# Softmax attentions with row sums from the value matmul and operand copies by DMA, in a two-block transformer step

## Chip, core and metric

The kernel runs on one core of a Trainium2 chip. The metric is the device time of one execution in microseconds (us).

## What is computed

Sequence 512, width 1024, batch 1, all in float32. The first block is one layer with two attention branches, a stick-breaking attention ("sb", 8 heads) and a latent attention ("mla", 8 heads of width 96, softmax over chunks of 64); the second has a softmax attention with forget-gate decay ("fox", 16 heads of 64), a short convolution, and two wide MLPs. The change touches the two softmax attentions. Cut to these:

```python
# mla: chunk-causal softmax, then the gate
z = einsum("bhqd,bshd->bhqs", q_blk, k) * scale
p = softmax(where(allowed, z, -inf), axis=-1)
o = einsum("bhqs,bshd->bhqd", p, v)
y_mla = (o * silu(gate_mla)) @ w_o_mla

# fox: causal softmax with cumulative log decay c
s = einsum("bhqd,bhkd->bhqk", q * HEAD_DIM ** -0.5, k)
s = s + c[..., :, None] - c[..., None, :]
s = where(k_pos <= q_pos, s, NEG_INF)
o = einsum("bhqk,bhkd->bhqd", softmax(s, axis=-1), v)
m = o @ w_out
```

## The kernel before, in words

Every product is made of split operands: a number is a high part (ScalarE's rounded copy) plus a low part (VectorE's difference), and `three` (L702 to L704) issues three matmuls for one product. Weights come in units of 1 MB: SP loads a unit into one of two raw slots (`load`, L490 and L491; it waits until the unit two places earlier has been split, `w_split`), ScalarE writes the high part (`w_hi`), VectorE the low part (`w_split`). Each engine runs its own stream in order, and semaphores alone tie the streams together.

The two softmax attentions run over pairs of heads: MLA 4 pairs, fox 8. What an engine does in a pair is written out by hand as an order of steps, one string for each engine (`PE_MLA`, `ACT_FOX` and so on; the last two pairs have strings of their own, `..._LAST`). A step is a letter and a number; for heads 0 and 1 of the pair the numbers 0 to 3 and 4 to 7 are query blocks of 128 rows, which see 128, 256, 384 and 512 keys:

- z: PE, scores of a block and the mask into one of three banks (L960, L964). For block 0 or 4 it waits until the head is staged.
- m: VectorE, negated row maximum (L1983). e: ScalarE, exponential with the row sum in an accumulator (L1412).
- n: VectorE, reciprocal of the sum (L1988) and P times it (L1991).
- t: PE, transposes of the block of P (L972). For s of 2 and more it waits for p of s - 2, since two banks take turns.
- p: high part of the turned P on ScalarE (L1421), low part on VectorE (L1694).
- v: PE, value product of a head, 12 matmuls, after p of its fourth block.
- g on PE: a share (6 matmuls of 512 columns) of a projection that runs beside, `beside`; its result is taken by x on VectorE (L1848) after the eighth share. u: the same for a second unit in the last pair.
- g on VectorE: `gather`, the head's output out of bank 5, in MLA times the gate (L1857, L1859).
- w on ScalarE, c on VectorE: the split of the unit beside which comes next, in two halves (L1190) and four quarters (L1658). c0 waits for `w_hi` of the whole unit, which w1 gives; `w_split` comes with c3.
- s on both: `stage` of the coming head, s1 of the pair's second head, s2 of the next pair's first. ScalarE writes high parts (L1288 to L1302), VectorE low parts. In fox ScalarE also writes second copies of q and k into the other half of the operand, and the decay rows picked out of `ssum` (L1293, L1294, L1298).
- o: split of a finished output tile for the output projection.

A fox pair p (0 to 7) has the unit `fox_qk_next` number p beside it in pairs 0 to 5 and splits number p + 1; pairs 6 and 7 have the output projection beside them. SP loads these units in a loop that holds nothing else. Behind the attention PE does the shares left of the output projection.

Of the kernel before, what the change touches and what calls it, by code (L numbers as in the profile page):

```python
# [208 lines left out]
def hybrid_block_kernel(nc, ins, out):  # L209
# [4 lines left out]
    with ctx:  # L214
        def sb(name, shape, dt=F32):
            return ctx.enter_context(nc.sbuf_tensor(name, shape, dt))
# [2149 lines left out]
```

## Time and profile before

| | us |
|---|---|
| median of 3 runs | 1865.53 (1863.59 to 1865.70) |
| profiled execution, time | 1864.47 |
| its span, first to last instruction | 1862.7 |
| PE busy | 1764.2 (95%) |
| VectorE busy | 1110.9 (60%) |
| ScalarE busy | 750.5 (40%) |
| GpSimd busy | 179.4 (10%) |
| granted clock of TensorE, mean | 0.986 |

The profile is one execution. Its times run from the span's start; the MLA attention lies at 324 to 415 us, the fox attention at 567 to 770. A matmul's row has its start and a modelled end, and a busy PE counts overlapping matmuls once. A window's row gives the stretch, its length, each engine's busy time with its number of instructions, the granted TensorE clock (1.00 is full speed), the mean busy share of the DMA engines and GB/s. "Idle before" is the idle time of an engine ahead of an instruction, with what ended it.

### The profile page before, as it was taken

The numbers are of one execution on the slowest core, as the hardware profiler recorded it, in microseconds if no ns is written. First come the engines' busy times: TensorE is split into PE (matmuls) and PEld (weight loads), VectorE is DVE, ScalarE is ACT, GpSimd is POOL, SyncE is SP. The second block draws the span as 40 slices with busy tenths as digits, with TensorE's granted clock in tenths as the row PEclk, the third lists the DMA queues.
The fourth block names the chain that finished last, engine by engine and source line by source line (L and its number), as shares of the span: only waits on it lengthen the run. The fifth ranks groups of instructions, "written<-read, shape, count | busy, mean of one in ns | idle before, by whom it ended". The sixth has DMA issues, their size and how long they took to land.

```text
span 1862.7 us, 22288 instructions
## 1 busy us (share of the span) xinstructions
PE 1764.2 (95%) x8332; PEld 1439.5 (77%) x8332; DVE 1110.9 (60%) x1580; ACT 750.5 (40%) x1169; POOL 179.4 (10%) x144
## 2 busy tenths in 40 slices
PE   8999999999898887989999999889999999999987
PEld 6988876888697675768888888667887788888866
DVE  6467767886556777675444453776556635354465
ACT  4266673554425667352222222642224322122245
POOL 2001110000300000140000001430003100000041
PEclk9999999999999998999999999989999999999999
DMA  7312133114231110223223222213222322322221
GB/s 248 95 48 68 48 70 102 46 46 137 67 91 46 46 45 1 91 68 113 90 97 106 90 91 95 86 45 113 94 99 68 114 90 96 106 91 90 86 68 62
DMA packets 162477, 156.23 MB, mean 84 GB/s; under 512 B 13602, under 2 KB 157247, under 8 KB 162143
## 3 DMA queue, kind: packets, MB, share of 16 engines
q1 hardware_dynamic: 162398, 155.16, 26.4%
q8 instruction: 52, 0.85, 0.2%
q14 instruction: 27, 0.21, 0.0%
HBM read 150.36 MB, written 4.19 MB: 83 GB/s over the span
## 4 chain that ended last, share of the span: by engine, by line
PE 65%; issue 13%; DVE 10%; ACT 5%; POOL 4%; DMA 1%; POOLq 0%; SPq 0%; DVEq 0%; ACTq 0%
PE bank L702 20%; PE bank L704 20%; PE bank L703 20%; POOL ssum L2296 3%; PE bank L972 1%; DVE act_b L1694 1%; PE bank L960 1%; DVE split_weights L1650 1%; DVE work L1709 1%; DVE negmax L1983 1%; POOL tmp L2329 1%; DVE act_a L1696 1%; DVE tmp L1991 1%; ACT split_weights L1181 1%; DMA raw_weights<-in_w_ple_gate 1%
## 5 line engine op out<-in xcount | busy, mean ns | idle before, releaser
L702 PE MATMUL bank<-act_a,split_weights 128*128 128x512 f32 x1392 | 557.5, 400 | 29.3 <-DVE act_a L1696 28.9
L704 PE MATMUL bank<-act_a,split_weights 128*128 128x512 f32 x1392 | 546.6, 393 | 0.0
L703 PE MATMUL bank<-act_a,split_weights 128*128 128x512 f32 x1392 | 546.0, 392 | 0.0
L1181 ACT ACTIVATE split_weights<-raw_weights 128x2048 fp32r<-128x2048 f32 (+1 forms) x119 | 223.7, 1880 | 343.7 <-PE bank L704 343.7
L1650 DVE TENSOR_TENSOR split_weights<-raw_weights,split_weights 128x2048 fp32r<-128x2048 f32 (+1 forms) x119 | 275.7, 2317 | 124.0 <-ACT split_weights L1181 120.6
L702 PEld LDWEIGHTS bank<-act_a,split_weights 128*128 128x128 f32 x1392 | 263.3, 189 | 94.0 <-issue 23.8
L704 PEld LDWEIGHTS bank<-act_a,split_weights 128*128 128x128 f32 x1392 | 262.7, 189 | 57.5
L703 PEld LDWEIGHTS bank<-act_a,split_weights 128*128 128x128 f32 x1392 | 263.3, 189 | 53.6 <-issue 2.2
L702 PE MATMUL bank<-act_b,split_weights 128*128 128x512 f32 x664 | 260.4, 392 | 0.0
L703 PE MATMUL bank<-act_b,split_weights 128*128 128x512 f32 x664 | 258.4, 389 | 0.0
L704 PE MATMUL bank<-act_b,split_weights 128*128 128x512 f32 x664 | 258.4, 389 | 0.0
L2300 POOL TENSOR_TENSOR ssum<-sq 128x512 f32<-128x512 f32 x16 | 28.0, 1750 | 1256.0 <-ACT sq L1211 1252.7
L702 PEld LDWEIGHTS bank<-act_b,split_weights 128*128 128x128 f32 x664 | 124.7, 188 | 26.8 <-issue 1.2
L703 PEld LDWEIGHTS bank<-act_b,split_weights 128*128 128x128 f32 x664 | 124.7, 188 | 26.8 <-issue 1.2
L704 PEld LDWEIGHTS bank<-act_b,split_weights 128*128 128x128 f32 x664 | 124.7, 188 | 26.0
L1518 ACT ACTIVATE act_b<-tmp 128x512 fp32r<-128x512 f32 x64 | 40.3, 632 | 229.3 <-DVE tmp L2157 227.9
L1211 ACT ACTIVATE sq<-work 128x512 f32<-128x512 f32 x117 | 71.0, 625 | 147.6 <-DVE work L2176 58.1
L2157 DVE SCALAR_TENSOR_TENSOR tmp<-bank,rstd 128x512 f32<-128x512 f32 x64 | 43.6, 691 | 137.2 <-PE bank L704 136.3
L2296 POOL TENSOR_TENSOR ssum<-ssum,sq 128x512 f32<-128x512 f32 x77 | 109.1, 1417 | 156.9 <-ACT sq L1211 148.5
L2176 DVE TENSOR_TENSOR work<-bank,work 128x512 f32<-128x512 f32 x48 | 32.9, 692 | 120.0 <-PE bank L704 120.0
L1694 DVE TENSOR_TENSOR act_b<-tmp,act_b 128x512 fp32r<-128x512 f32 (+3 forms) x136 | 77.4, 605 | 10.7 <-ACT act_b L480 9.3
L1412 ACT ACTIVATE tmp<-bank,negmax 128x128 f32<-128x128 f32 (+1 forms) x96 | 50.4, 526 | 56.3 <-DVE negmax L1983 56.3
(193 smaller groups left out, 2126.0 us busy)
## 6 DMA issues: line engine op xcount, KB each, us to landing
raw_weights<-in_w_mlp_up SPq DMA_DIRECT2D x32, 1024.0 KB, 5.4
raw_weights<-in_w_mlp_down SPq DMA_DIRECT2D x32, 1024.0 KB, 5.1
raw_weights<-in_w_in SPq DMA_DIRECT2D x20, 1024.0 KB, 5.3
raw_weights<-in_w_conv_in SPq DMA_DIRECT2D x12, 1024.0 KB, 5.1
raw_weights<-in_w_attn_in SPq DMA_DIRECT2D x16, 512.0 KB, 4.5
raw_weights<-in_w_ple_gate SPq DMA_DIRECT2D x8, 1024.0 KB, 5.2
raw_weights<-in_w_out SPq DMA_DIRECT2D x4, 1024.0 KB, 5.1
raw_weights<-in_w_attn_in SPq DMA_DIRECT2D x4, 1024.0 KB, 5.2
```

Source lines behind the costliest of these rows:

```text
L702: nc.tensor.matmul(dst, w[0], a[0], start=first, stop=False)
L703: nc.tensor.matmul(dst, w[0], a[1], start=False, stop=False)
L704: mm = nc.tensor.matmul(dst, w[1], a[0], start=False, stop=last)
L1181: nc.scalar.activation(wsp[:, pl.slot, 0, pl.split_cols], raw[:, pl.slot, pl.raw_cols], ACT.Copy)\
L1211: nc.scalar.activation(sq[:, parity, :], src, ACT.Square).then_inc(sq_done, 1)
L1412: nc.scalar.activation(tmp[:, s % 4, 0:(j + 1) * P], score_bank(s, last)[:, 0:(j + 1) * P], ACT.Exp, bias=negmax[:, s:s + 1], accum_out=ro ...
L1518: nc.scalar.activation(act_b[:, 0, 2 * j + m, :], tmp[:, m, :], ACT.Square)\
L1650: V.tensor_tensor(wsp[:, pl.slot, 1, cols], raw[:, pl.slot, pl.raw_cols], wsp[:, pl.slot, 0, cols].bitcast(F32), ALU.subtract).then_inc(w_ ...
L1694: V.tensor_tensor(dst, src, hi.bitcast(F32), ALU.subtract).then_inc(sem_, 1)
L2157: V.scalar_tensor_tensor(out=tmp[:, m, :], in0=done(pl, m)[:, :], scalar=0.0, in1=rstd[:, :], op0=ALU.max, op1=ALU.mult).then_inc(tile_rea ...
L2176: V.tensor_tensor(t, done(pl, m)[:, :], t, ALU.add).then_inc(tile_read, 1)
L2296: nc.gpsimd.tensor_tensor(ssum[:, :], ssum[:, :], sq[:, parity, :], ALU.add).then_inc(sq_added, 1)
```

## The change

Row sums and normalisation. `head_v` becomes twice as wide, V's 64 columns and 64 more that hold 1.0 in the high part and 0.0 in the low part, set once. The value product then has 128 output rows: rows 64 to 127 of bank 5 are the row sums, 64 times. P is turned as the exponential gives it. A new step r on ScalarE (`invert_sums`) takes Ln and Exp with scale -1 of the sums into a half of `sq`, and `gather` multiplies by that; in MLA the gate is a multiplication of its own for both heads.

Staging in fox. ScalarE makes three copies a head instead of six (`HI_STEPS` 3). SP makes the second copies of q and k and the two decay rows with four DMAs a head (`copy_halves`), and PE waits for them (`halves_copied`) at the head's first scores.

The orders of all engines in MLA and fox are written anew (the PE orders of the last two fox pairs stay).

```diff
-        head_v = sb("head_v", [P, 2, 2, TT, HD], F32R)
+        head_v = sb("head_v", [P, 2, 2, TT, 2 * HD], F32R)
-        HI_STEPS = {"sb": 4, "mla": 3, "fox": 6}
+        HI_STEPS = {"sb": 4, "mla": 3, "fox": 3}
-        PE_MLA = "z0 z1 g0 z2 t0 g1 z3 t1 g2 z4 t2 z5 g3 t3 z6 t4 z7 v0 t5 g4 g5 t6 t7 g6 g7 v1"
-        PE_FOX = "z0  z1 g0 z2 t0 g1 z3 t1 g2 z4 t2 z5 g3 t3 z6 t4 z7 v0 t5 g4 g5 t6 t7 g6 g7 v1"
-        ACT_MLA = "s1 e0 e1 e2 p0 e3 p1 w0 e4 p2 e5 p3 w1 e6 s2 p4 p5 e7 p6 p7"
-        ACT_FOX = "s1  e0 e1 e2 p0 e3 p1 w0 e4 p2 e5 p3 w1 e6 s2 p4 p5 e7 p6 p7"
-        DVE_MLA = "m0 m1 n0 s1 m2 n1 m3 n2 p0 p1 n3 m4 m5 p2 n4 p3 n5 m6 c0 n6 m7 c1 p4 c2 g0 n7 p5 c3 s2 p6 p7 x0 x1 g1"
-        DVE_FOX = "m0  m1 n0 s1 m2 n1 m3 n2 p0 p1 n3 m4 m5 p2 n4 p3 n5 m6 c0 n6 m7 c1 p4 c2 g0 n7 p5 c3 s2 p6 p7 x0 x1 g1"
+        PE_MLA = "z0 z1 z2 g0 g1 t0 z3 g2 t1 z4 t2 z5 g3 t3 z6 g4 v0 t4 z7 t5 g5 t6 t7 g6 g7 v1"
+        ACT_MLA = "s1 e0 e1 p0 e2 w0 w1 p1 p2 e3 e4 p3 e5 e6 s2 r0 p4 p5 e7 p6 p7 r1"
+        DVE_MLA = "m0 m1 m2 s1 p0 m3 c0 m4 p1 m5 c1 p2 c2 p3 m6 m7 p4 p5 p6 g0 p7 s2 x0 x1 c3 g1"
+        PE_FOX = "z0 z1 z2 g0 g1 t0 z3 t1 g2 z4 t2 t3 z5 g3 t4 v0 z6 t5 z7 g4 g5 t6 t7 g6 g7 v1"
+        ACT_FOX = "s1 e0 e1 p0 e2 p1 e3 p2 p3 e4 e5 s2 p4 p5 w0 e6 e7 r0 p6 p7 w1 r1"
+        DVE_FOX = "m0 m1 m2 s1 m3 p0 p1 m4 p2 p3 m5 s2 m6 p4 m7 p5 c0 c1 g0 p6 p7 x0 c2 x1 c3 g1"
-        ACT_LAST = ("s1 e0 e1 e2 o0 p0 w0 e3 o1 p1 p2 o2 w1 e4 e5 p3 s2 e6 p4 e7 p5 p6 p7 o3",
-                    "s1 e0 e1 e2 o4 p0 p1 e3 o5 e4 p2 p3 e5 e6 p4 p5 o6 e7 p6 p7")
-        DVE_LAST = ("m0 n0 m1 m2 n1 s1 n2 m3 p0 o0 m4 p1 n3 m5 o1 p2 p3 n4 c0 m6 n5 o2 g0 n6 c1 p4 m7 c2 n7 p5 s2 c3 p6 p7 o3 g1",
-                    "m0 m1 n0 m2 s1 n1 n2 o4 p0 p1 m3 m4 n3 m5 o5 n4 p2 p3 n5 m6 n6 m7 g0 p4 n7 o6 p5 p6 p7 g1")
-        ACT_MLA_LAST = "e0 s1 e1 e2 p0 e3 p1 w0 e4 p2 e5 p3 w1 e6 p4 e7 p5 o0 o1 p6 p7 o2"
-        DVE_MLA_LAST = "m0 m1 n0 s1 m2 n1 m3 p0 n2 p1 m4 n3 m5 p2 n4 p3 n5 m6 c0 n6 m7 c1 p4 c2 g0 n7 p5 c3 o0 p6 o1 p7 x0 x1 o2 g1"
+        ACT_LAST = ("s1 e0 e1 e2 o0 p0 w0 e3 o1 p1 p2 o2 w1 e4 e5 p3 s2 e6 p4 r0 e7 p5 p6 p7 o3 r1",
+                    "s1 e0 e1 e2 o4 p0 p1 e3 o5 e4 p2 p3 e5 e6 p4 p5 r0 o6 e7 p6 p7 r1")
+        DVE_LAST = ("m0 m1 m2 s1 m3 p0 o0 m4 p1 m5 o1 p2 p3 c0 m6 o2 c1 p4 m7 g0 c2 p5 s2 c3 p6 p7 o3 g1",
+                    "m0 m1 m2 s1 o4 p0 p1 m3 m4 m5 o5 p2 p3 m6 m7 p4 p5 g0 o6 p6 p7 g1")
+        ACT_MLA_LAST = "s1 e0 e1 p0 e2 w0 w1 p1 p2 e3 e4 p3 e5 e6 r0 p4 o0 p5 e7 o1 p6 p7 o2 r1"
+        DVE_MLA_LAST = "m0 m1 m2 s1 p0 m3 c0 m4 p1 m5 c1 p2 c2 p3 m6 m7 p4 o0 p5 g0 o1 p6 c3 p7 x0 x1 o2 g1"
             loop("fox_v", 2, 2, lambda i, j: attn_in[:, :, bass.ds(2 * D + 512 * i + 256 * j, 256)])
-            with sp.Fori(0, 3) as i:
-                for j in range(2):
-                    load_qk(Place(tab, "fox_qk_next", j, i, 2, 3), 2 + 2 * i + j)
+            def copy_halves(h):
+                hh = h % 2
+                qk, (own, other) = qk_parts("fox", hh), halves(hh)
+                sp.wait_ge(ATT["fox"]["stage_hi"], HI_STEPS["fox"] * h + 2)
+                for dst, src in ((qk(0)[other, :], qk(0)[own, :]), (qk(3)[own, :], qk(2)[own, :])):
+                    sp.dma_start(dst.bitcast(F32), src.bitcast(F32)).then_inc(halves_copied[hh], 16)
+                for part in range(2):
+                    row, to = 32 * part + h, other.start + part
+                    sp.dma_start(qk(3)[to:to + 1, :].bitcast(F32), ssum[row:row + 1, :]).then_inc(halves_copied[hh], 16)
             for j in range(2):
-                pl = Place(tab, "fox_out", j)
-                load_out(pl, j)
+                load_qk(Place(tab, "fox_qk_next", j), 2 + j)
+            sp.wait_ge(forget_log, 4)
+            sp.wait_ge(pad_zero, 3)
+            copy_halves(0)
+            load_qk(Place(tab, "fox_qk_next", 2), 4)
+            for pair in range(FOX_HEADS // 2):
+                copy_halves(2 * pair + 1)
+                if pair < 3:
+                    load_qk(Place(tab, "fox_qk_next", 3 + pair), 5 + pair)
+                elif pair < 5:
+                    load_out(Place(tab, "fox_out", pair - 3), pair - 3)
+                if pair < FOX_HEADS // 2 - 1:
+                    copy_halves(2 * pair + 2)
...
                     if j == 0:
                         pe.wait_ge(A["staged"], 3 * (2 * i + hh) + 3)
+                        if kind == "fox":
+                            pe.wait_ge(halves_copied[hh], 64 * i + 64)
...
                 def turn(i, s):
-                    pe.wait_ge(A["normed"], 8 * i + s + 1)
+                    pe.wait_ge(A["exp"], 8 * i + s + 1)
...
-                        three(banks[5][0:HD, c:S], [head_v[:, hh, hl, kt, :] for hl in (0, 1)],
+                        three(banks[5][:, c:S], [head_v[:, hh, hl, kt, :] for hl in (0, 1)],
...
-                if kind == "fox":
-                    nc.scalar.activation(qk(0)[other, :], q, ACT.Copy, scale=scale).then_inc(A["stage_hi"], 1)
-                    nc.scalar.activation(qk(3)[own, :], k, ACT.Copy).then_inc(A["stage_hi"], 1)
-                    if first:
-                        act.wait_ge(pad_zero, 3)
-                    pick = consts[0:48, bass.ds(ccols["sel"].start + 2 * i + hh, 1)]
-                    nc.scalar.activation(qk(3)[other.start:other.start + 48, :], decay_parts, ACT.Copy, scale=pick)\
-                        .then_inc(A["stage_hi"], 1)
...
-                                         bias=negmax[:, s:s + 1], accum_out=rowsum[:, s:s + 1]).then_inc(A["exp"], 1)
+                                         bias=negmax[:, s:s + 1]).then_inc(A["exp"], 1)
+
+                def invert_sums(i, hh):
+
+                    h = 2 * i + hh
+                    act.wait_ge(A["out"], FREE + h + 1)
+                    nc.scalar.activation(sum_inverse(hh), banks[5][HD:2 * HD, :], ACT.Ln).then_inc(A["sum_log"], 1)
+                    act.wait_ge(A["sum_log"], h + 1)
+                    nc.scalar.activation(sum_inverse(hh), sum_inverse(hh), ACT.Exp, scale=-1.0).then_inc(A["sum_inverse"], 1)
...
-                if kind == "fox":
-                    V.tensor_scalar(dst, src, 1.0, None, ALU.mult).then_inc(A["gathered"], 1)
+                if kind != "sb":
+                    dve.wait_ge(A["sum_inverse"], 2 * i + hh + 1)
+                    V.tensor_tensor(dst, src, sum_inverse(hh), ALU.mult).then_inc(A["gathered"], 1)
+                    if kind == "mla" and hh == 1:
+                        dve.wait_ge(A["gathered"], FREE + 2 * i + 2)
+                        V.tensor_tensor(output_tile(kind, i), output_tile(kind, i), wt(TILES[kind]["gate"] + i), ALU.mult)\
+                            .then_inc(A["gated"], 1)
...
-                def normalize(i, s):
-                    dve.wait_ge(A["exp"], 8 * i + s + 1)
-                    V.reciprocal(rinv[:, s:s + 1], rowsum[:, s:s + 1]).then_inc(A["step"], 1)
-                    dve.wait_ge(A["step"], 8 * i + s + 1)
-                    t = tmp[:, s % 4, 0:(s % TT + 1) * P]
-                    V.tensor_scalar(t, t, rinv[:, s:s + 1], None, ALU.mult).then_inc(A["normed"], 1)
```

## Rows read from the trace of the kernel before

**Rows 1.** The page's busy time of each engine, its share of the span, instructions
```profile
PE 1764.2 (95%) x8332; PEld 1439.5 (77%) x8332; DVE 1110.9 (60%) x1580; ACT 750.5 (40%) x1169; POOL 179.4 (10%) x144
```

**Rows 2.** Table of windows, one MLA pair, then fox pairs 0, 1, 2, 6, 7
```profile
core 0: us, PE busy (x) PEld busy (x) DVE busy (x) ACT busy (x) POOL busy (x), PEclk, DMA share, GB/s
324.00:346.60 22.60, 22.11 (x124) 18.52 (x125) 18.04 (x45) 13.11 (x34) 0.00 (x0) 1.00 0.19 58
...
567.30:595.00 27.70, 22.92 (x115) 18.24 (x116) 18.74 (x45) 19.35 (x43) 0.00 (x0) 0.94 0.15 39
595.00:619.40 24.40, 21.56 (x118) 17.11 (x117) 19.16 (x46) 16.45 (x38) 0.00 (x0) 1.00 0.15 40
619.40:645.20 25.80, 22.99 (x118) 18.36 (x117) 19.35 (x46) 16.43 (x38) 0.00 (x0) 0.93 0.17 45
...
718.50:745.80 27.30, 18.57 (x89) 13.95 (x88) 20.37 (x48) 18.39 (x42) 0.00 (x0) 0.81 0.00 1
745.80:770.00 24.20, 21.12 (x110) 16.59 (x107) 15.93 (x41) 9.65 (x28) 0.00 (x0) 0.93 0.34 109
```

**Rows 3.** Waits of PE, 595 to 717: waiter, releaser, us in total, times, longest
```profile
PE bank L972 <- DVE act_b L1694: 11.3, 10, 1.6
```

**Rows 4.** Lines by form, VectorE, one fox pair: count, busy us, mean ns, idle before
```profile
L1988 DVE RECIPROCAL rinv<-rowsum 128x1 f32<-128x1 f32 x8 | 1.2, 155 | 0.3 <-ACT tmp L1412 0.2
...
L1991 DVE TENSOR_SCALAR tmp<-tmp,rinv 128x512 f32<-128x512 f32 x2 | 1.0, 488 | 0.1
...
L1991 DVE TENSOR_SCALAR tmp<-tmp,rinv 128x128 f32<-128x128 f32 x2 | 0.6, 286 | 0.1
```

**Rows 5.** Lines by form, ScalarE, the same fox pair
```profile
L1190 ACT ACTIVATE split_weights<-raw_weights 128x1024 fp32r<-128x1024 f32 x2 | 2.1, 1054 | 0.0
L1412 ACT ACTIVATION_READ_ACCUMULATOR tmp<-bank,negmax 128x1 f32 x8 | 1.6, 197 | 0.0
...
L1421 ACT ACTIVATE act_b<-bank 128x512 fp32r<-128x512 f32 x2 | 1.2, 598 | 2.3 <-PE bank L972 2.3
...
L1298 ACT ACTIVATE act_b<-ssum,consts 48x512 fp32r<-48x512 f32 x1 | 0.7, 723 | 0.0
...
L1293 ACT ACTIVATE head_qk<-work 64x512 fp32r x1 | 0.6, 632 | 0.0
```

**Rows 6.** Timeline of SP, 589.0 to 590.5: start, us, DMAs issued
```profile
589.32 1.00 SPq L491 DMA_DIRECT2D raw_weights<-in_w_attn_in  x2
```

**Rows 7.** Timeline of SP, 286 to 292: start, us, DMAs issued
```profile
286.64 4.95 SPq L569 DMA_DIRECT2D work<-tmp  x8
```

**Rows 8.** The page's DMA issues: count, KB each, median us from issue to landing
```profile
work<-tmp SPq DMA_DIRECT2D x8, 64.0 KB, 2.0
```

**Rows 9.** DMA view, 589.0 to 595.0: busy tenths in 40 slices
```profile
DMA  0000000002664779999999999999999999610200
```

**Rows 10.** Timeline of VectorE, 658 to 670: start, us, operation
```profile
662.04 0.68 DVE L1658 TENSOR_TENSOR split_weights<-raw_weights,split_weights 128x512 fp32r<-128x512 f32 x1
662.64 0.68 DVE L1857 TENSOR_SCALAR work<-bank 64x512 f32 x1
...
666.53 1.15 DVE L1694 TENSOR_TENSOR act_b<-bank,act_b 128x384 fp32r<-128x384 f32 x2
```

**Rows 11.** Timeline of PE, 1230 to 1244: start, us, [idle before <-releaser]
```profile
1238.24 0.76 PE L702 MATMUL bank<-act_a,split_weights 128*128 128x512 f32 x1 [6.04 <-DVE act_a L1696]
1238.80 0.63 PE L703 MATMUL bank<-act_a,split_weights 128*128 128x512 f32 x1
1239.22 0.63 PE L704 MATMUL bank<-act_a,split_weights 128*128 128x512 f32 x1
...
1243.76 0.39 PE L703 MATMUL bank<-act_a,split_weights 128*128 128x512 f32 x1
1243.98 0.40 PE L704 MATMUL bank<-act_a,split_weights 128*128 128x512 f32 x1
```

**Rows 12.** Table of windows, columns as in rows 2
```profile
1238.20:1243.50 5.30, 5.26 (x13) 4.13 (x14) 5.30 (x6) 2.67 (x6) 2.73 (x2) 0.50 0.00 0
```

More of the change, by code:

```diff
@@ L246, in hybrid_block_kernel @@
         negmax = sb("negmax", [P, 8])
-        rowsum = sb("rowsum", [P, 8])
-        rinv = sb("rinv", [P, 8])
         banks = [ctx.enter_context(nc.psum_tensor(f"bank{i}", [P, S], F32)) for i in range(8)]
@@ L337, in hybrid_block_kernel @@
                 "part_ready", "summed", "w_exp", "negmax", "exp", "normed", "pt_hi", "pt_ready",
-                "out", "gathered", "o_hi", "o_ready", "step")}
+                "out", "sum_log", "sum_inverse", "gathered", "gated", "o_hi", "o_ready")}
+        halves_copied = [sem("halves_copied0"), sem("halves_copied1")]
         block = ctx.enter_context(nc.Block())
@@ L427, in halves, with sum_inverse @@
             return slice(hh * HD, (hh + 1) * HD), slice((1 - hh) * HD, (2 - hh) * HD)
+        def sum_inverse(hh):
+            return sq[hh * HD:(hh + 1) * HD, 0, :]
         def head_values(kind, i, hh):
@@ L908, in _ @@
                         c = min(kt * P, S - 2 * P)
-                        three(banks[4 + hh][0:HD, c:S], [head_v[:, hh, hl, kt, :] for hl in (0, 1)],
+                        three(banks[4 + hh][0:HD, c:S], [head_v[:, hh, hl, kt, 0:HD] for hl in (0, 1)],
                               [act_b[:, hl, kt, c:S] for hl in (0, 1)], kt == 0, kt == TT - 1,
@@ L1291, in stage @@
                     nc.scalar.activation(qk(2)[other, :], k, ACT.Copy).then_inc(A["stage_hi"], 1)
-                if kind == "fox":
-                    nc.scalar.activation(qk(0)[other, :], q, ACT.Copy, scale=scale).then_inc(A["stage_hi"], 1)
-                    nc.scalar.activation(qk(3)[own, :], k, ACT.Copy).then_inc(A["stage_hi"], 1)
-                    if first:
-                        act.wait_ge(pad_zero, 3)
-                    pick = consts[0:48, bass.ds(ccols["sel"].start + 2 * i + hh, 1)]
-                    nc.scalar.activation(qk(3)[other.start:other.start + 48, :], decay_parts, ACT.Copy, scale=pick)\
-                        .then_inc(A["stage_hi"], 1)
                 if not first:
                     act.wait_ge(A["out"], FREE + 2 * i + hh - 1)
-                nc.scalar.activation(head_v[:, hh, 0, :, :], head_values(kind, i, hh), ACT.Copy).then_inc(A["stage_hi"], 1)
+                nc.scalar.activation(head_v[:, hh, 0, :, 0:HD], head_values(kind, i, hh), ACT.Copy).then_inc(A["stage_hi"], 1)
             table("sigmoid_and_others")
@@ L1349, in output_hi @@
             def output_hi(kind, k):
-                act.wait_ge(ATT[kind]["gathered"], FREE + 2 * k + 2)
+                if kind == "mla":
+                    act.wait_ge(ATT[kind]["gated"], k + 1)
+                else:
+                    act.wait_ge(ATT[kind]["gathered"], FREE + 2 * k + 2)
                 nc.scalar.activation(out_parts(kind, 0, k), output_tile(kind, k), ACT.Copy).then_inc(ATT[kind]["o_hi"], 1)
@@ L1435, in two_pairs @@
                                 output_hi(kind, s)
+                            elif what == "r":
+                                invert_sums(pair, s)
                             elif what == "e":
@@ L1820, in stage @@
                 dve.wait_ge(A["stage_hi"], before + HI_STEPS[kind])
-                low(head_v[:, hh, 1, :, :], head_values(kind, i, hh), head_v[:, hh, 0, :, :], A["staged"])
+                low(head_v[:, hh, 1, :, 0:HD], head_values(kind, i, hh), head_v[:, hh, 0, :, 0:HD], A["staged"])
             def rest_halves(part, value):
@@ L1836, in _ @@
                     rest_halves(3, 0.0)
+                    for hl, value in ((0, 1.0), (1, 0.0)):
+                        V.memset(head_v[:, :, hl, :, HD:2 * HD].bitcast(F32), value)
                     clear_padding()
@@ L2024, in two_pairs @@
                             else:
-                                {"n": normalize, "p": turned_lo}[what](pair, s)
+                                turned_lo(pair, s)
                 passes = BESIDE_PASSES[kind]
@@ L2103, in _ @@
             n.add("step")
-            chain(V.tensor_tensor(decay_parts[32:32 + FOX_HEADS, :], total, hi, ALU.subtract))
+            V.tensor_tensor(decay_parts[32:32 + FOX_HEADS, :].bitcast(F32R), total, hi, ALU.subtract).then_inc(forget_log, 1)
             rest_halves(1, 1.0)
```

## Prediction

> **What bounds the kernel now.** I read the page's busy line first: TensorE is busy for 1764 of 1862.7 us [rows 1], so only its idle time, and time at the lower clock, can be won or lost. Then I cut the two softmax attentions into pairs of heads, from the first scores step (z0) of a pair to that of the next, and read the table of windows [rows 2]. An MLA pair takes 22.6 us with PE busy for 22.1: nothing is left there. A steady fox pair takes 24.4 us with PE busy for 21.56, 2.8 us idle. Over five fox pairs transposes (L972) wait ten times for VectorE's low part of an earlier turned P, 11.3 us [rows 3] of the 14 us that PE is idle in them. Two fox pairs are longer for another reason: in 619.4 to 645.2 the granted clock is 0.93 and the pair takes 25.8. The seventh pair (718.5 to 745.8) has few beside matmuls, PE is busy for 18.6 of 27.3 us at clock 0.81: there the chain through VectorE and ScalarE is the bound. All six pairs with beside work together are 567.3 to 718.5, 151.2 us; the last two 51.5.
>
> **What the change removes.** Per pair, VectorE loses eight reciprocals (0.155 us each) and eight multiplications of P (0.29 for 128 columns to 0.49 for 512), some 4.3 us [rows 4]. ScalarE loses eight accumulator reads (0.197 each, 1.6 us) and in fox three of the six staging copies of each head (0.63, 0.63 and 0.72), 4.0 us a pair [rows 5]. It gains two operations of 64x512 per head (Ln and Exp of the sums, about 0.65 each by the 64x512 copy's 0.63), 2.6 us a pair. VectorE gains in MLA one 128x512 multiplication per pair (0.68). On TensorE the value matmuls keep their columns; they load 128 instead of 64 weight columns under a matmul that is longer, which I take as nothing: loads are busy for 18.5 us where matmuls are for 22.1 [rows 2], 0.15 us each, so even if the 24 loads of a pair took twice as long they would fit beside the matmuls. Bounds 0 and, if half of that lay bare, 1.8 us an MLA pair (in fox it falls under the stalls below). Could all this be cashed in, it would be at most the idle 2.8 us of each of six fox pairs, 17 us, a further 5 us of lower clock, and a few us in the last two.
>
> **The edit that decides: where SyncE issues the copies.** In fox a head's second operand copies (two DMAs of 64x512) and its decay rows (two of 1x512) are now issued by SP, which works in order: copies of head 2p+1, then the weight unit 3+p of pair p (waits until the slot's old unit is split), then the copies of head 2p+2. The slot's old unit is index 1+p, and its last quarter is split by c3 of pair p. So in pairs 0 to 4 the copies for the next pair's first head stand behind c3 and two 512 KB load DMAs. The trace shows that the load waits there: SP issues it at 589.32, when c3 of the first pair is done, 5.7 us ahead of the next pair at 595.0 [rows 2, 6]. In the new VectorE order c3 comes behind x0, c2 and x1, and x0 waits for the last beside matmul (g7), behind which PE has only v1. The scores of the next pair wait for `halves_copied`, so PE stands still from the end of v1 until the copies have landed, with everything else queued behind z0.
>
> The time from c3 to the landing isn't in the trace; its parts are. Two loads take SP 1.0 us to issue [rows 6]. Eight SBUF-to-SBUF DMAs (64 KB each) take it 4.95 us, 0.62 each, and each lands 2.0 us after its issue [rows 7, 8]. If the engines ran them side by side with the load, the last copy would be issued at 1.05 + 3 x 0.62 = 2.9 and land at 4.9 us. If they come after the load: in the stretch from 589.0 to 595.0 the DMA engines are busy with the 1.05 MB from the tenth to the 35th slice of 0.15 us [rows 9], so until 4.9 us after the issue, at 277 GB/s; 0.26 MB more is 0.95, and with an estimated 0.6 to the semaphore it is 6.5. I take the middle, 5.7, and keep 4.9 and 6.5. The Trainium skill (DMA: Bandwidth & Descriptors, Queues, rings and completion order) says that each DMA engine takes descriptors in ring order and that a semaphore's increment lands after all earlier writes of that engine. By it the value would be the 6.5, and the sum 4 us more. It speaks against this place for the copies; no row before has such copies right behind a load, so it is open here.
>
> **Second cost: c0 behind w1.** VectorE's `split_share` waits at share 0 for the unit's whole high part, that is for w1 on ScalarE, and the change leaves that as it is. The new fox order of ScalarE has w1 behind p7 and before r1; VectorE has c0, c1, g0, p6, p7 in this order. So v1, which needs p7 and g0, waits for: t7, high part of p7 (0.60), w1 (1.05 [rows 5]), c0, c1, g0, low p6, low p7. VectorE's operations of 512 columns follow each other by 0.60 us though each is 0.68, and low p6 and p7 take 1.15 together [rows 10], so the five take 3 x 0.60 + 1.15 = 2.95. With three handovers of 0.1 it is 4.9 us from the end of t7 to v1. PE has g6 and g7 in that time, 12 matmuls at 0.22 to 0.23 from start to start at full clock [rows 11], 2.7. Left: 2.2 us of idle, in each of six pairs. Bounds: 1.0 (ScalarE's parts hidden) and 3.3 (0.68 for each, and Ln and Exp of r0 late).
>
> **The new fox pair.** I went through the new orders with these durations. With n gone no transpose waits in the first part: after a late z0, PE has z1, z2, g0 and g1 (about 3.6 us) for m0 and e0, which need 0.9; t2, t4 and t6 find their low parts done. So z0 to g7 is PE's work alone, 21.56 less 2.0 for v1, 19.5 us. v1 starts at 21.7 and ends at 23.8. Low p7 ends at 21.6, x0, c2, x1, c3 at 24.0. SP wakes at 24.1, and the copies are there at 29.8. So PE idles for 6.0 us at the end of v1 on top of the 2.2, where before it idled 2.8 in all.
>
> **Clock.** After 6.04 us of idle PE the granted clock is 0.50, the lower level of 1.2 GHz, for another 5.3 us of matmuls, which start 0.42 instead of 0.22 us apart [rows 11, 12]: 2.5 us lost. The shortest drop is that of the fox pair at 0.93, 25.8 against 24.4: 1.4 lost [rows 2]. I take 2.2 us per stall of this kind, bounds 0 and 5 (in the seventh pair before, 0.19 of 27.3 us, that is 10 us at half clock). For the pair without the copy stall (the sixth) another 1.0 because v1 comes after an idle time.
>
> Pair 0: 29.8. Pairs 1 to 4: 29.8 + 2.2 = 32.0 each, 128.0. Pair 5 has no load ahead of its copies: 23.8 + 2.2 + 1.0 = 27.0. Together 184.8 against 151.2, **+33.6 us**.
>
> **The rest.** Pairs 6 and 7: the copies are issued as soon as ScalarE has staged; they land 2.4 + 2.0 = 4.4 us later, and z4 comes 6 us or more after z0. VectorE loses 4.3 us in each. But in pair 6 c, s, o and p stay, t0 and t2 wait for m0 behind r1 and the new g1 (1.3 us more), and v0 waits for low p3 behind ScalarE's o, w and e. My walk gives 26 and 24 for the old 27.3 and 24.2: -1.5, bounds -6 and +2. MLA: PE is the bound and stays it. g1 has Ln, Exp and the gate in front of the next m0, but z0, z1, z2, g0, g1 (4.3 us) cover the 3.9 us until e0 is done; v0 and t7 may wait 0.4 each. 0 for four pairs, bounds -2 and +4. Behind fox the last output tile comes 1.3 us later; three beside matmul shares and the transposes stand between: +0.3, bounds 0 and 1.3. Two memsets for the ones, once, beside PE's projections: 0, at most 1.2. Together -1. The sum is +32.6 on the profiled execution's 1864.5 us (span 1862.7), which is 1 us under the median of 1865.5: **1897**.
>
> **Rivals.**
> - *The copies are late but c0 costs nothing* (ScalarE reaches w1 early enough, bound 0). c3 is then at 19.5 + 0.1 + 2.4 = 22.0, z0 at 27.8, pair 5 at 22.7: 2.0 x 5 + 4 = 14 less, 1883. Against it: w1 stands behind p7 and t7 in both written orders. 0.12.
> - *The clock stays low in the fox part.* PE would be busy for 68% of the pair, as in the seventh pair before, where the clock was 0.81: 5 us per stall, 2.8 x 5 = 14 more, 1911. For it: three gaps in a pair. Against it: after each long gap above the clock was back at 5.3 us. 0.10.
> - *Faster: the copies land before z0.* It needs SP to be past the load's wait by the time v1 starts, c3 some 4 us earlier than g7 allows. If the copy DMAs of the next head did not stand behind c3 at all, a pair would be 23.8: 6 x 23.8 + 1 = 143.8, -7.4, with the -1 1856. It decides at c3 ending 5.7 us before v1's end. The code's order of SP and the wait of the load until 589.32 [rows 6] speak against it. 0.08.
>
> **The numbers.** Forecast 0.70. The range takes both slow rivals and the bounds: 5 x (-0.8 or +0.8) for the landing, 6 x (-1.2 or +1.1) for c0, 5 x (-2.2 or +2.8) for the clock and the few us of the rest, which seldom fall together: 1879 to 1914. Outside lie the fast case and about 0.1 of the tails. 0.2% is 4 us, about what a measurement of this kernel can tell. Faster 0.08 (the fast case), same 0.02, slower 0.90.
>
> **What would show it.** Right: before z0 of fox pairs 1 to 5 PE is idle for 5 to 7 us and the releaser is a DMA; SP's load starts after v1 has ended and the copies right behind it; VectorE's split of the share at c0 waits for ScalarE's L1190, some 2 us before v1; low clock after each stall; pairs of 30 to 32 us, then one of 27; MLA pairs still 22 to 23. Wrong: fox pairs of 21 to 24 us with L972 no longer waiting, or a landing of the copies well before c3, or c0 ahead of t7.

## The result, and the profile after

| | before, us | after, us |
|---|---|---|
| median | 1865.0 (4 runs) | 1896.55 (4 runs, 1896.25 to 1897.70) |
| span of the profiled execution | 1862.7 | 1895.9 |
| PE busy | 1764.2 | 1770.2 |
| VectorE busy | 1110.9 | 1069.8 |
| ScalarE busy | 750.5 | 739.6 |
| granted clock, mean | 0.986 | 0.975 |

The ratio is 1.0171, 95% interval 1.0154 to 1.0189: the change makes the kernel 1.7% slower, 32 us, although VectorE has 41 us and ScalarE 11 us less to do. The table of windows of the kernel after, cut at the z0 of each pair as in [rows 2]; the columns are those named in its first line:

```profile
core 0: us, PE busy (x) PEld busy (x) DVE busy (x) ACT busy (x) POOL busy (x), PEclk, DMA share, GB/s
325.20:347.40 22.20, 22.20 (x124) 19.10 (x125) 14.06 (x29) 12.80 (x26) 0.00 (x0) 1.00 0.05 16
...
567.40:598.80 31.40, 21.46 (x117) 18.28 (x118) 15.56 (x30) 15.63 (x31) 0.00 (x0) 0.92 0.24 59
598.80:632.30 33.50, 23.58 (x117) 20.02 (x118) 15.57 (x30) 14.29 (x28) 0.00 (x0) 0.86 0.19 48
632.30:666.30 34.00, 23.86 (x117) 20.25 (x118) 15.57 (x30) 14.30 (x28) 0.00 (x0) 0.85 0.18 47
666.30:699.80 33.50, 23.96 (x117) 20.33 (x118) 15.57 (x30) 14.29 (x28) 0.00 (x0) 0.86 0.17 47
699.80:731.90 32.10, 23.12 (x117) 19.76 (x118) 15.56 (x30) 14.29 (x28) 0.00 (x0) 0.82 0.17 49
731.90:756.90 25.00, 23.07 (x115) 19.72 (x116) 14.53 (x29) 11.62 (x23) 0.00 (x0) 0.90 0.05 11
756.90:782.40 25.50, 18.46 (x88) 15.03 (x87) 16.96 (x33) 15.79 (x32) 0.00 (x0) 0.80 0.10 22
```

The first row is an MLA pair, 22.2 us where it was 22.6, and PE is now never idle in it. Then come fox pairs 0 to 6. Pairs 0 to 4 take 31.4 to 34.0 us instead of 24.4 to 27.7. PE is busy for 21.5 of the 31.4 us of pair 0, so some 10 us are idle; in pairs 1 to 4 it is busy for 1.7 to 2.5 us more, at a granted clock of 0.82 to 0.86. Pair 5 is back at 25.0. The waits of PE from 598 to 733 (who waits, for whom, us in total, times, longest):

```profile
PE bank L984 <- DMA head_qk<-ssum: 38.8, 5, 8.2
PE bank L724 <- DVE act_b L1723: 7.7, 4, 1.9
```

The transposes' wait for VectorE's low parts, 11.3 us in five pairs before [rows 3], is gone. In its place stand two others: the scores of a new pair (L984) wait five times for the copy of a decay row, 38.8 us, and the value product (L724 on `act_b`) four times for VectorE, 1.9 us each. How the second pair ends, on the timeline of PE (start, length, idle before it in brackets):

```profile
619.54 0.39 PE L726 MATMUL bank<-act_a,split_weights 128*128 128x512 f32 x1
621.86 0.49 PE L724 MATMUL bank<-act_b,head_v 128*128 128x512 f32 x1 [1.93 <-DVE act_b L1723]
...
623.78 0.28 PE L726 MATMUL bank<-act_b,head_v 128*128 128x256 f32 x1
632.05 0.80 PE L984 MATMUL bank<-head_qk 128*128 128x256 f32 x2 [7.99 <-DMA head_qk<-ssum]
...
634.35 0.63 PE L724 MATMUL bank<-act_a,split_weights 128*128 128x512 f32 x1
634.77 0.63 PE L725 MATMUL bank<-act_a,split_weights 128*128 128x512 f32 x1
```

The last beside matmul starts at 619.54 and v1 at 621.86, after 1.93 us of idle; v1 ends at 624.1 and z0 starts at 632.05, after 7.99 us. The matmuls behind it start 0.42 us apart, as in [rows 11]: the lower clock of 1.2 GHz. VectorE in the same stretch, c0 with c1, and c3:

```profile
618.78 1.29 DVE L1687 TENSOR_TENSOR split_weights<-raw_weights,split_weights 128x512 fp32r<-128x512 f32 x2 [3.67 <-ACT split_weights L1214]
...
623.45 0.67 DVE L1687 TENSOR_TENSOR split_weights<-raw_weights,split_weights 128x512 fp32r<-128x512 f32 x1
```

and ScalarE's high parts of p6 and p7, and w1:

```profile
616.80 0.99 ACT L1448 ACTIVATE act_b<-bank 128x384 fp32r<-128x384 f32 x2
617.69 1.05 ACT L1214 ACTIVATE split_weights<-raw_weights 128x1024 fp32r<-128x1024 f32 x1
```

c0 waits 3.67 us for w1, which runs behind p7 from 617.69 to 618.74; c3 ends at 624.12. Then SP, which stood at this load, waiting for c3:

```profile
624.20 1.00 SPq L494 DMA_DIRECT2D raw_weights<-in_w_attn_in  x2
625.24 2.06 SPq L645 DMA_DIRECT2D head_qk<-head_qk  x2
627.34 1.24 SPq L648 DMA_DIRECT2D head_qk<-ssum  x2
```

The two load DMAs go out at 624.20, 0.08 us behind c3, and the four copies of the next head behind them. The last lands at 632.0, when z0 starts.

### The profile page after: what moved, and what is told of

Read it like the earlier page. It is cut to its first block, busy times and chain, and to the rows that moved or that the text cites. A ratio compares the mean times of both kernels' runs of the same rounds, so it can differ in the third digit from the quotient of the medians.

```text
span 1895.9 us, 22068 instructions
## 1 busy us (share of the span) xinstructions
PE 1770.2 (93%) x8332; PEld 1456.2 (77%) x8332; DVE 1069.8 (56%) x1394; ACT 739.6 (39%) x1073; POOL 179.3 (9%) x144
## 4 chain that ended last, share of the span: by engine, by line
PE 68%; issue 12%; DVE 7%; POOL 4%; ACT 4%; DMA 3%; SPq 1%; POOLq 0%; DVEq 0%; ACTq 0%
PE bank L724 21%; PE bank L726 21%; PE bank L725 21%; POOL ssum L2325 3%; PE bank L984 2%; PE bank L996 1%; DMA head_qk<-ssum 1%; DVE split_weights L1679 1%; DVE work L1738 1%; DVE act_b L1723 1%; POOL tmp L2358 1%; DVE act_a L1725 1%; ACT split_weights L1205 1%; PE bank L988 1%; DMA raw_weights<-in_w_mlp_up 1%
## 5 line engine op out<-in xcount | busy, mean ns | idle before, releaser
L724 PE MATMUL bank<-act_a,split_weights 128*128 128x512 f32 x1392 | 558.1, 401 | 27.9 <-DVE act_a L1725 27.5
L724 PEld LDWEIGHTS bank<-act_a,split_weights 128*128 128x128 f32 x1392 | 264.8, 190 | 93.8 <-issue 23.0
L724 PE MATMUL bank<-act_b,split_weights 128*128 128x512 f32 x664 | 260.4, 392 | 0.0
L724 PEld LDWEIGHTS bank<-act_b,split_weights 128*128 128x128 f32 x664 | 124.6, 188 | 26.8 <-issue 1.2
L2019 DVE TENSOR_REDUCE negmax<-bank 128x1 f32<-128x128 f32 (+1 forms) x96 | 45.7, 485 | 77.0 <-PE bank L988 76.8
```

What stands on the lines that cost most here:

```text
L724: nc.tensor.matmul(dst, w[0], a[0], start=first, stop=False)
L2019: V.reduce_max(negmax[:, s:s + 1], score_bank(s, last)[:, 0:(s % TT + 1) * P], AX, negate=True)\
```

## The experiments

All times are medians of four runs on a chip that also ran the kernel before; its median there was 1864.2 to 1864.9. "Pairs" are fox pairs.

### Copies ahead of the load

```diff
                 copy_halves(2 * pair + 1)
+                if pair < FOX_HEADS // 2 - 1:
+                    copy_halves(2 * pair + 2)
                 if pair < 3:
                     load_qk(Place(tab, "fox_qk_next", 3 + pair), 5 + pair)
                 elif pair < 5:
                     load_out(Place(tab, "fox_out", pair - 3), pair - 3)
-                if pair < FOX_HEADS // 2 - 1:
-                    copy_halves(2 * pair + 2)
```

> Only SyncE's order is changed: the copies of the next pair's first head are issued ahead of the weight load of the pair, so that they no longer stand behind the load's wait for c3. Theory (the stall of PE before z0 is the place of the copies in SP's order): the five waits of 7.3 to 8.4 us before z0 go, the low clock behind them too; fox pairs 0 to 5 take 23.4 to 24.5 us each, some 142 in all instead of 189.5, and v1 still waits 1.9 us for VectorE. Time 1849 us. Rival (the four copy DMAs are slow in themselves, some 4 us from issue to landing, and hold up z0 or z4 wherever they stand): 1875 to 1885, with a wait for a DMA of 3 to 5 us left in each pair.

Measured: 1851.5 us (ratio to the kernel before 0.993, 0.991 to 0.995). The windows of pairs 0, 1 and 2, and two of PE's waits from 598 to 730:

```profile
566.30:590.50 24.20, 22.17 (x117) 19.16 (x118) 14.88 (x29) 12.97 (x26) 0.00 (x0) 0.95 0.10 23
590.50:615.20 24.70, 22.77 (x117) 19.48 (x116) 15.31 (x30) 14.20 (x28) 0.00 (x0) 0.91 0.26 65
615.20:638.00 22.80, 20.87 (x117) 17.77 (x117) 14.84 (x30) 14.20 (x28) 0.00 (x0) 1.00 0.28 69
```

```profile
PE bank L724 <- DVE act_b L1723: 10.4, 6, 1.9
...
PE bank L984 <- DMA act_b<-ssum: 2.4, 3, 1.4
```

Six pairs take 143.3 us instead of 189.5. No z0 of theirs waits any more. What is left in them is v1's wait of 1.93 us in each (five of the six waits of L724 in this stretch; the sixth, 0.8 us, is pair 6's) and at most 1.4 us for the second head's copies (`act_b`). The granted clock is still low in two pairs: pair 1 has PE busy for 22.8 us at 0.91, pair 2 for 20.9 at 1.00, although v1 waits 1.93 us in both. This one move of two lines is worth 45 us, more than the whole slowdown.

### w1 behind w0

```diff
-        ACT_FOX = "s1 e0 e1 p0 e2 p1 e3 p2 p3 e4 e5 s2 p4 p5 w0 e6 e7 r0 p6 p7 w1 r1"
+        ACT_FOX = "s1 e0 e1 p0 e2 p1 e3 p2 p3 e4 e5 s2 p4 p5 w0 w1 e6 e7 r0 p6 p7 r1"
```

> Only ScalarE's fox order is changed: w1 stands right behind w0 instead of behind p7, so that c0 no longer waits behind t7. Theory: the 1.9 us of idle before v1 go in six pairs, c3 and the load come 1.9 us earlier with v1, the stall before z0 stays at 7.3 to 8.4: 1896.5 - 6 x 1.9 = 1885 us. Rival (e6 and e7 come 1 us later behind w1, t6 and t7 wait, and the chain of p7 takes the gain back): 1893 to 1898, with a wait of PE for e6 or e7.

Measured: 1883.2 us (1.010, 1.008 to 1.011). On the timeline of PE from 590 to 630 only these two instructions have idle time before them:

```profile
595.96 0.80 PE L984 MATMUL bank<-head_qk 128*128 128x256 f32 x2 [7.62 <-DMA head_qk<-ssum]
...
626.39 0.79 PE L984 MATMUL bank<-head_qk 128*128 128x256 f32 x2 [7.70 <-DMA head_qk<-ssum]
```

v1's wait is gone, z0's is still 7.6 to 7.9 us in all five pairs. The window of pair 5, in which there is neither:

```profile
718.80:741.20 22.40, 22.40 (x116) 19.44 (x116) 14.71 (x29) 11.59 (x23) 0.00 (x0) 0.91 0.05 12
```

It takes 22.4 us with PE busy throughout, its first part still at the low clock behind its own late z0 (0.91 over the pair). The gain is 13.3 us, 2.2 a pair; e6 and e7, 1 us later now, hold up nothing.

### Both

The two diffs above together.

> Both edits: copies ahead of the load, w1 behind w0. Theory: they add up, since one stall lies before v1 and the other before z0: 1896.5 - 47 - 11 = 1838 us, fox pairs 0 to 5 at 21.5 to 22.5, and below both kernels. Rival: with the long stall gone VectorE's chain g1, m0, e0 behind r1 comes late for t0, or p7 for v1, and 4 to 6 us of the sum are lost: 1843.

Measured: 1838.1 us (0.986, 0.985 to 0.988). The two edits were worth 45.0 and 13.3 us alone and are worth 58.5 together: they add up. The windows of pairs 0 and 1, and the only wait for a DMA from 598 to 730:

```profile
567.00:587.80 20.80, 20.79 (x116) 17.97 (x117) 14.66 (x29) 12.90 (x26) 0.00 (x0) 1.00 0.12 26
587.80:609.80 22.00, 20.84 (x118) 17.82 (x117) 15.33 (x31) 14.15 (x28) 0.00 (x0) 1.00 0.29 73
```

```profile
PE bank L984 <- DMA act_b<-ssum: 3.3, 4, 1.3
```

Pair 0 is 20.8 us of uninterrupted PE work. Pair 1 has 1.2 us of idle, z4's wait for the second head's copies; these are still issued behind the load.

### Copies behind c3, but ahead of the load's DMAs

```diff
                 copy_halves(2 * pair + 1)
+                if pair < 5:
+                    sp.wait_ge(w_split, tab.first["fox_qk_next"] + 3 + pair - 1)
+                if pair < FOX_HEADS // 2 - 1:
+                    copy_halves(2 * pair + 2)
                 if pair < 3:
```

(with the same call behind the load taken out)

> SyncE first waits for c3 as the load does, then issues the four copies, and only then the two load DMAs. Ring order (the copies wait in the DMA queues behind the 1 MB of the load): now the last copy lands 2.4 + 2.0 us behind c3, so the stall before z0 is 4.5 instead of 7.3 to 8.4, five times, and the clock is low for a little less: 1896.5 - 5 x 3.5 - 2 = 1877 us. Rival (SP's issue and the copies' own time make the 7.9 us from c3 to the landing, whatever goes ahead of them): 1891 to 1896.

Measured: 1876.1 us (1.006, 1.004 to 1.008). SP, and the next z0 on PE:

```profile
619.12 1.14 SPq L645 DMA_DIRECT2D head_qk<-head_qk  x2
620.30 1.23 SPq L648 DMA_DIRECT2D head_qk<-ssum  x2
621.63 1.15 SPq L494 DMA_DIRECT2D raw_weights<-in_w_attn_in  x2
```

```profile
622.72 0.78 PE L986 MATMUL bank<-head_qk 128*128 128x256 f32 x2 [3.70 <-DMA head_qk<-ssum]
```

The copies go out where the load went before, at once behind c3, and the last lands 3.6 us later: this z0 waits 3.70 instead of 7.99 us, and the five together wait 16.9 instead of 38.8. The 21.9 us less of idle time gave 20.4 us; the clock gave nothing back, for PE is busy for 22.7 to 23.8 us in pairs 1 to 4 here too. The DMA view gives the median time from issue to landing of the same four copies; first in this kernel, then in the changed one (head_qk, the four behind the load):

```profile
head_qk<-head_qk SPq DMA_DIRECT2D x2, 128.0 KB, 2.2
...
head_qk<-ssum SPq DMA_DIRECT2D x2, 2.0 KB, 1.8
```

```profile
head_qk<-head_qk SPq DMA_DIRECT2D x2, 128.0 KB, 4.9
...
head_qk<-ssum SPq DMA_DIRECT2D x2, 2.0 KB, 4.0
```

2.2 and 1.8 us alone, 4.9 and 4.0 us behind the load. And they land in the order of their issue: in the second pair of the changed kernel the load's second DMA lands at 630.55 and the four copies at 630.63, 631.11, 631.40 and 632.00, the first of them 5.4 us after its issue. So the copies queue behind the load's data and do not run beside it. Of the 7.9 us from c3 to the landing 3.6 are the copies' own, and 4.3 come from the megabyte ahead of them, 1.0 of it the issue of the two load DMAs.

### The load one pair later

```diff
             for pair in range(FOX_HEADS // 2):
                 copy_halves(2 * pair + 1)
-                if pair < 3:
-                    load_qk(Place(tab, "fox_qk_next", 3 + pair), 5 + pair)
-                elif pair < 5:
-                    load_out(Place(tab, "fox_out", pair - 3), pair - 3)
+                if 1 <= pair < 4:
+                    load_qk(Place(tab, "fox_qk_next", 2 + pair), 4 + pair)
+                elif 4 <= pair < 6:
+                    load_out(Place(tab, "fox_out", pair - 4), pair - 4)
```

(beside w1 behind w0)

> As the last one with both edits (w1 behind w0, copies not behind c3), but each weight load stands one pair later in SyncE's order, behind the copies of the pair's second head, so that these don't queue behind the load's 1 MB either. Theory (ring order): the waits of z4 for the second head's copies (up to 1.3 us, 3.3 us in pairs 1 to 5) go, nothing else changes, since the unit is needed only a pair later: 1838 - 3 to 4 = 1834 us. Rival (the later load comes late for w0, or z4's wait only moves to t4 or v0 behind it): 1838 to 1842.

Measured: 1834.5 us (0.984, 0.982 to 0.986). Windows of pairs 0, 1, 2 and 6:

```profile
567.20:588.00 20.80, 20.80 (x116) 17.98 (x117) 14.69 (x29) 12.89 (x26) 0.00 (x0) 1.00 0.12 26
588.00:608.70 20.70, 20.70 (x118) 17.86 (x118) 15.38 (x31) 14.17 (x28) 0.00 (x0) 1.00 0.31 77
608.70:629.50 20.80, 20.80 (x118) 17.92 (x118) 15.43 (x31) 14.17 (x28) 0.00 (x0) 1.00 0.30 76
691.70:718.70 27.00, 18.91 (x88) 15.50 (x88) 16.91 (x33) 15.81 (x32) 0.00 (x0) 0.81 0.09 21
```

Pairs 0 to 5 are now 20.7 to 20.8 us each with PE busy for all of it at full clock: PE has no idle time left there. Pair 6 remains, 27.0 us with PE busy for 18.9. It is longer than in the run with both edits, where it took 24.7 us with the same order and nearly the same idle time; there the granted clock was 0.86, here 0.81. So 2.3 us of the 5.5 that the first six pairs gained against that run went again in pair 6.

### The sums without the DMA copies

```diff
-        HI_STEPS = {"sb": 4, "mla": 3, "fox": 3}
+        HI_STEPS = {"sb": 4, "mla": 3, "fox": 6}
+                if kind == "fox":
+                    nc.scalar.activation(qk(0)[other, :], q, ACT.Copy, scale=scale).then_inc(A["stage_hi"], 1)
+                    nc.scalar.activation(qk(3)[own, :], k, ACT.Copy).then_inc(A["stage_hi"], 1)
...
-                        if kind == "fox":
-                            pe.wait_ge(halves_copied[hh], 64 * i + 64)
```

> The row sums and the new orders with w1 behind w0, but fox operand copies and decay rows on ScalarE as in the kernel before; no copy DMAs, and SyncE's old loop. Shows what the DMA copies are worth beside the sums. Theory (ScalarE's staging stands ahead of e0 and of p4, p5, e6 in its order, so that 2.0 us more a head come onto the chain of t0 and of t6): 2 to 3 us in each of eight pairs more than with the DMA copies, 1855 to 1862 us. Rival (ScalarE is busy for only half of a pair, its copies are hidden): 1838 to 1842 us.

Measured: 1852.7 us (0.994, 0.992 to 0.996), 14.7 us more than with the copies by DMA. On PE's timeline of one pair:

```profile
618.16 0.33 PE L975 MATMUL bank<-consts,tmp 128*128 128x128 f32 x1 [1.20 <-ACT tmp L1418]
...
630.39 1.23 PE L975 MATMUL bank<-consts,tmp 128*128 128x128 f32 x7 [0.79 <-ACT tmp L1418]
```

t0 waits for e0, which stands behind the six steps of s1, and t6 for e6, behind those of s2. Pairs take 23.4 us. So ScalarE's copies weren't hidden, although it is busy for only 17.9 us of a pair: they stood ahead of operations that PE waits for.

### The DMA copies alone

```diff
-                    nc.scalar.activation(qk(0)[other, :], q, ACT.Copy, scale=scale).then_inc(A["stage_hi"], 1)
-                    nc.scalar.activation(qk(3)[own, :], k, ACT.Copy).then_inc(A["stage_hi"], 1)
...
+                copy_halves(2 * pair + 1)
+                if pair < FOX_HEADS // 2 - 1:
+                    copy_halves(2 * pair + 2)
...
+                            pe.wait_ge(halves_copied[hh], 64 * i + 64)
```

> The kernel before with one part of the change alone: fox operand copies and decay rows by DMA, issued ahead of the load; normalisation and orders as before. Theory (in the kernel before, VectorE's low p4 waits 1.9 us for ScalarE's high p4, which stands behind the six staging copies of s2; with three of them gone the waits of t6 and t7, 0.66 and 1.60 a pair, go, and the low clock of two pairs): 6 x 2.2 + 3 = 16 less than before, 1849 us. Rival (VectorE with its 19 us a pair is what the transposes wait for; ScalarE's copies are hidden): 1862 to 1866 us.

Measured: 1848.9 us (0.992, 0.990 to 0.994). The transposes' waits from 590 to 700:

```profile
PE bank L994 <- DVE act_b L1708: 2.3, 5, 0.5
PE bank L994 <- DVE tmp L2005: 1.5, 5, 0.3
```

In nearly five pairs the transposes wait 3.8 us for VectorE; in the kernel before, L972's wait was 11.3 us in five [rows 3]. Pairs take 22.4 us instead of 24.4, with no low clock. What looked like a wait for VectorE was ScalarE's. In the kernel before, low p4 on VectorE waits for high p4, and ScalarE comes to that only when the six steps of s2 are through (the last of them is L1302):

```profile
661.83 0.29 DVE L1694 TENSOR_TENSOR act_b<-bank,act_b 128x128 fp32r<-128x128 f32 x1 [1.89 <-ACT act_b L1421]
```

```profile
661.22 0.42 ACT L1302 ACTIVATE head_v<-work 128x256 fp32r x1
661.54 0.53 ACT L1421 ACTIVATE act_b<-bank 128x128 fp32r<-128x128 f32 x2
```

The two halves of the change are worth 16.0 us (this one) and 12.1 (the run above, both against the kernel before), 26.7 together, a little less than their sum.

### The old step orders

The orders of MLA and fox as in the kernel before, without n, r0 ahead of e7 and r1 at the end; copies ahead of the load.

```diff
+        PE_FOX = "z0 z1 g0 z2 t0 g1 z3 t1 g2 z4 t2 z5 g3 t3 z6 t4 z7 v0 t5 g4 g5 t6 t7 g6 g7 v1"
+        ACT_FOX = "s1 e0 e1 e2 p0 e3 p1 w0 e4 p2 e5 p3 w1 e6 s2 p4 p5 r0 e7 p6 p7 r1"
+        DVE_FOX = "m0 m1 s1 m2 m3 p0 p1 m4 m5 p2 p3 m6 c0 m7 c1 p4 c2 g0 p5 c3 s2 p6 p7 x0 x1 g1"
```

> The changed kernel with the copies ahead of the load, but with the step orders of the kernel before in MLA and fox (n dropped, r0 put ahead of e7, r1 at the end; the orders of the last two fox pairs stay the changed ones). Shows what the new orders are worth. Theory (the gain comes from the work removed, not from the orders; the old orders put only z0, z1, g0, z2 ahead of t0, while e0 now waits behind r1, g1, m0, s1, so t0 waits some 0.5 to 1 us a pair): 1842 to 1846 us. Rival (the new orders carry the gain): 1851 or more, as the same kernel with the new orders and the late w1.

Measured: 1848.1 us (0.991, 0.990 to 0.993), between the two expectations. PE's timeline of one pair has

```profile
617.10 0.33 PE L996 MATMUL bank<-consts,tmp 128*128 128x128 f32 x1 [0.68 <-ACT tmp L1431]
...
631.11 0.63 PE L996 MATMUL bank<-consts,tmp 128*128 128x128 f32 x4 [0.35 <-DVE act_b L1723]
```

and 0.25 us before a v: 1.3 us a fox pair, which then takes 22.8 us, and MLA pairs of 22.5 to 23.1 instead of 22.2. With w1 early the new orders bring 10 us (1838.1); with w1 late, as the change has them, they are 3.4 us behind the old ones (1851.5): the misplaced w1 takes back more than the rest of the new orders gives.

### The seventh pair

```diff
-        PE_LAST = ("z0 z1 t0 z2 t1 z3 t2 z4 z5 t3 z6 t4 v0 g0 t5 z7 t6 g1 t7 g2 v1",
+        PE_LAST = ("z0 z1 z2 t0 z3 t1 z4 t2 z5 t3 z6 t4 z7 v0 g0 t5 t6 g1 t7 g2 v1",
```

(z2 ahead of t0 and z7 ahead of v0; e6 ahead of s2 on ScalarE too; the rest as with the later load)

> As the run with the later load, and in the seventh fox pair (p = 6) z2 goes ahead of t0, z7 ahead of v0 and e6 ahead of s2. In the run before, PE idles there for 6.8 us: 2.5 before t0, 1.9 and 0.5 for low parts, 1.1 before v0, 0.7 before t7. Theory (these waits are partly of order, m2 and m7 wait behind them for z2 and z7): 2 to 3 us less, 1832 us. Rival (the pair is bound by the work of VectorE and ScalarE and by r1, g1, m0 at its start, not by PE's order): 1834 to 1836 us.

Measured: 1831.8 us (0.982, 0.981 to 0.984), the fastest of all. The pair takes 24.0 instead of 27.0 us. PE's first two waits in it:

```profile
695.80 0.33 PE L996 MATMUL bank<-consts,tmp 128*128 128x128 f32 x1 [2.02 <-ACT tmp L1431]
...
699.23 0.76 PE L984 MATMUL bank<-act_b 128*128 128x256 f32 x2 [2.11 <-DMA act_b<-ssum]
```

z4 now waits 2.1 us for its copies, which it did not before: it comes earlier than they do. The idle time named in PE's waits of this pair fell from 8.1 to 6.8 us only. The clock did the rest: PE is busy for 17.2 us at 0.86 here and for 18.9 at 0.81 in the run before. With the old order of this pair and a clock of 0.86, the run with both edits had it at 24.7 us. So the kernel is 2.7 us faster, but it is not shown that the order is worth 2 to 3 us: at the same clock the pair gained 0.7, and what brought the higher clock is open.

## Why the prediction was right, step by step

It said 1897 us and slower with 0.90; 1896.55 were measured. By its own steps:

- **Where the copies stand.** Right in place and kind: five z0, of pairs 1 to 5, wait for a DMA; SP's load starts 0.08 us behind c3, and c3 ends when v1 does. Moving the copies took the stall away and 45 us with it; its price is thus shown, clock included, not argued. In the six pairs it is 46 us: 38.8 of idle time and 9.7 of PE busy, most of that clock, less the 2.4 that z4 now waits.
- **From c3 to the landing** the sum had 5.7 us, between 4.9 and 6.5. It measured 7.9 in the second pair and 7.5 to 8.2 in the five, outside the bounds: this is the term that was mis-sized, by 2.1 x 5, some 10 us. The lower bound (copies beside the load) is refuted by 4.9 and 4.0 us to landing behind the load and 2.2 and 1.8 ahead of it. The rule of the Trainium skill (DMA: Bandwidth & Descriptors, Queues, rings and completion order), descriptors taken in ring order, was the better guide, and the trace agrees with it: the copies land in their order, the first of them from 0.1 us ahead to 0.2 us behind the load's second DMA. The upper bound was too low in both of its parts. In the second pair the load's second DMA landed 6.35 us after the load's issue, where the sum had 4.9 + 0.6 and the kernel before has 5.55; the last copy landed 1.45 us behind it, where the sum had 0.95. Why the load is slower to land with copies queued behind it no run shows.
- **c0 behind w1.** 2.2 us forecast, 1.93 measured in each pair, with the chain as told: w1 behind p7, c0, c1, g0, p6, p7. The run with w1 early gave 13.3 us back, 2.2 a pair, where 6 x 1.93 is 11.6.
- **The pair without its stalls.** 23.8 us to the end of v1 forecast; pair 0 has 23.1 (its next z0 at 598.5, less 8.0 of idle, less 567.4). In six pairs that is 4 us too much. 0.3 a pair is v1's wait; the rest came from taking PE busy of a pair before, 21.56, as pure work: it is 20.7 when nothing interrupts it. c3 was too late by the same, and it came with the end of v1, not 0.2 us behind it.
- **Clock.** 2.2 us a stall forecast; beyond 23.1 and the wait for the copies pairs 1 to 5 take 2.0 to 2.8 us each. The 1.0 more for v1 of pair 5 did not come; pair 5 took 25.0 for 27.0. The five together are 12.1 us for a forecast of 12.0.
- **Sum of pairs 0 to 5:** 189.5 for 184.8 (151.2 before). It divides without a rest into 6 x 23.1 (4 us under the forecast), 38.8 us of idle before z0 (forecast 5 x 6.0, so 9 more) and the clock's 12.1 (as forecast).
- **The rest** was put at -1; it was -5. The time from z0 of pair 6 to the end of the kernel fell by 5.2 us: 1.8 in pair 6, 0.6 in pair 7 and 2.8 behind it, which no run explains. MLA pairs are shorter by 0.4 each, but the first of them starts 1.2 us later, so the fox part starts where it did. The memsets cost nothing: VectorE's step ahead of them comes 1.0 us late, and so does the one behind them. That the pairs came out 5 us over and the rest 4 under the forecast is what brought the sum back to within 1 us: the exact hit is in part luck of two errors of opposite sign.
- **The signs.** Two of them came out beyond what was named: PE idles for 7.0 to 8.2 us before z0, not 5 to 7, and pairs 1 to 4 take up to 34.0 us, not 32. The mechanism is the one foretold, its size was taken too small.
- **The rivals.** A c0 for nothing and a clock that stays low did not happen. The fast case, 1856, was built on the copies landing in time with c0 as it is; the run that does this gave 1851.5. In the case of a free c0 the 22.7 us for pair 5 is a slip of the sum: 19.5 + 2.0 + 2.2 is 23.7, and the case would be 1884.

## What to carry to other kernels

An in-order DMA queue that also waits for buffers is part of the critical path: before adding a DMA to it, ask what the instruction ahead waits for, when that comes, and how much data goes out between; small DMAs that someone waits for go ahead of large loads, which can wait a stage. The same holds for an engine that is half idle: what counts is what stands behind the added or removed work in its order, not its busy share. And a wait is only as early as the event that raises it: c0 reads only what w0 has written and waited for the flag that w1 gives. (A flag of w0's own was not tried; only w1 was moved.)

## What the runs showed of the hardware

- SP's issue of a DMA right behind a 1 MB load is held up: the first two copies take 2.06 us to issue behind it, the next two 1.24, and the first two 1.14 when the queue is empty (the load's own two take 1.00). Over the five pairs the four copies take 2.8 to 3.3 us to issue behind the load, where they take 2.4 without one. The issuing engine, not the DMA engines alone, is late then.
- A DMA of one row of 2 KB lands hardly sooner than one of 128 KB: 1.8 us against 2.2 with no load ahead of it. Four DMAs a head cost SP 2.4 us of issue whatever their size.
- TensorE without idle time does a fox pair in 20.7 us where 21.56 us of busy time had been counted with gaps. PE's busy time of a pair at full clock grows with its gaps: 20.7 us with none (later load), 20.9 with one and 21.1 with two (copies ahead of the load), 21.4 with two (copies on ScalarE), 21.4 and 21.55 with three (DMA copies alone, old orders), 21.56 with four (before). Some of each gap is thus counted as work: the last matmul before v1's wait is shown for 0.39 us where starts follow each other by 0.23, and v1's first is followed after 0.33. So the gain from closing gaps is larger than the idle time shown: a steady pair went from 24.4 to 20.75 us, 3.7 for 2.8 us of idle.
- The same idle time lowers TensorE's clock in one pair and not in the next. With the copies ahead of the load v1 waits 1.93 us in all six pairs; behind it the granted clock falls to 0.50 in pairs 0 and 1 and stays full in pairs 2 to 5. In the changed kernel each of the five waits of 7.0 to 8.2 us comes with the low clock, and with the copies between c3 and the load so do the five of 2.8 to 3.7 us; v1's wait lies just ahead of each, so what the shorter wait alone would do to the clock is not shown.
